# PEER experts of a two-layer decoder step: gathered rows, or both tables streamed through TensorE

## The reference

```python
q = (xt @ w_q).reshape(n, PEER_HEADS, 2, PEER_QDIM // 2)
s = jnp.einsum('nhcd,hckd->nhck', q, sub_keys).astype(jnp.float32)
s1, i1 = lax.top_k(s[:, :, 0], PEER_TOPK)
s2, i2 = lax.top_k(s[:, :, 1], PEER_TOPK)
...
top, sel = lax.top_k(cand, PEER_TOPK)
eidx = jnp.take_along_axis(cidx, sel, axis=-1)
gate = jax.nn.softmax(top, axis=-1)
...
a = jax.nn.gelu(jnp.einsum('nhkd,nd->nhk', u[ek], xk).astype(jnp.float32), approximate=False)
return jnp.einsum('nhk,nhkd->nd', (gk * a).astype(v.dtype), v[ek])
```

## Time and profile before

| | |
|---|---|
| median of 3 runs | 2763.49 us (2759.49 to 2781.48) |
| profiled execution, first to last instruction | 2750.8 us |
| PE busy | 2018.4 us (73%), 6651 matmuls |
| DVE busy | 1539.8 us (56%) |
| ACT busy | 415.0 us (15%) |
| POOL busy | 692.8 us (25%) |
| DMA | 759.36 MB, of which 608.21 MB by the gathers |
| mean granted TensorE clock | 0.828 |

### The profile page before, as it was taken

One profiled execution on the slowest core, in us unless ns is written; L12 is line 12 of the kernel. 1 busy time (PEld: TensorE's weight loads), 2 busy tenths in 40 slices (PEclk: granted clock), 3 DMA queues, 4 the chain that ended last, 5 costly groups with the idle time before them and its releaser, 6 DMA issues. The chain is left out here.

```text
span 2750.8 us, 21320 instructions
## 1 busy us (share of the span) xinstructions
PE 2018.4 (73%) x6651; PEld 989.5 (36%) x6651; DVE 1539.8 (56%) x3816; ACT 415.0 (15%) x1168; POOL 692.8 (25%) x612
## 2 busy tenths in 40 slices
PE   8956688895666867779786766776867767666766
PEld 3544446372122233334452332531223344222222
DVE  0063431377987453433559366488377647966665
ACT  0000231001111011111111122111123111111111
POOL 4000000002232222222232132233133424244542
PEclk9975565997888987778788988898988889888888
DMA  8201001437688897777887989997988999699997
GB/s 277 78 1 21 14 1 53 162 123 298 227 329 308 332 353 275 286 291 278 292 311 276 348 311 364 361 360 270 399 328 338 409 392 368 244 407 421 422 419 296
DMA packets 190137, 759.36 MB, mean 276 GB/s; under 512 B 22204, under 2 KB 79432, under 8 KB 116168
## 3 DMA queue, kind: packets, MB, share of 16 engines
q0 software_dynamic: 84480, 608.21, 56.5%
q1 hardware_dynamic: 105544, 149.80, 15.9%
HBM read 752.35 MB, written 5.60 MB: 276 GB/s over the span
## 5 line engine op out<-in xcount | busy, mean ns | idle before, releaser
L1750 PE MATMUL ps<-uv,diag 128*128 128x512 f32 (+1 forms) x1884 | 1059.4, 705 | 373.0 <-ACT diag L1726 339.7
L1638 POOL DMA_INDIRECT uv<-in_experts_dram,slots x576 | 662.2, 1150 | 1993.9 <-PE ps L1750 1332.6
L1658 DVE CUSTOM_DVE_ANT_0 uv<-uv,x 128x1024 f32<-128x1024 f32 x512 | 622.9, 1223 | 305.6 <-DMA uv<-in_experts_dram,slots 176.0
L1750 PEld LDWEIGHTS ps<-uv,diag 128*128 128x128 f32 (+1 forms) x1884 | 368.9, 210 | 940.3 <-ACT diag L1726 453.7
L1726 ACT ACTIVATE diag<-const,wgt 128x128 f32<-128x128 f32 (+1 forms) x471 | 164.2, 385 | 810.6 <-DVE wgt L1668 779.6
L1713 ACT ACTIVATE gelu<-dot 128x2 f32<-128x2 f32 x288 | 58.6, 203 | 673.7 <-DVE dot L1658 668.3
L1680 DVE SCALAR_TENSOR_TENSOR acc<-uv,wgt,acc 128x1024 f32<-128x1024 f32 x100 | 128.1, 1281 | 0.0
L421 PE MATMUL ps<-even_w,xT 128*128 128x512 f32 (+3 forms) x240 | 96.9, 559 | 0.9 <-DMA even_w<-in_even_w_in_dram 0.9
L1658 DVE CUSTOM_DVE_ANT_0 uv<-uv,xs 128x1024 f32<-128x1024 f32 x64 | 78.3, 1226 | 29.1 <-DMA ffn_gb<-in_ln_ffn_b_dram 14.0
L704 PE MATMUL ps<-sample_s_kTs,sample_s_q_b 64*32 64x256 f32 x256 | 62.2, 414 | 43.9 <-DVEq L1782 43.9
L421 PEld LDWEIGHTS ps<-even_w,xT 128*128 128x128 f32 (+1 forms) x240 | 37.5, 163 | 59.9 <-issue 56.1
(11 more groups left out here) (414 smaller groups left out, 2109.5 us busy)
## 6 DMA issues: line engine op xcount, KB each, us to landing
uv<-in_peer_w_q_dram SPq DMA_DIRECT2D x16, 1024.0 KB, 11.9
sample_cache<-in_cache_dil_kv_dram SPq DMA_DIRECT2D x64, 256.0 KB, 8.6
sample_cache<-in_odd_w_in_dram SPq DMA_DIRECT2D x12, 1024.0 KB, 8.5
first_w<-in_odd_w_in_dram SPq DMA_DIRECT2D x12, 1024.0 KB, 9.6
last_w<-in_odd_w_in_dram SPq DMA_DIRECT2D x12, 1024.0 KB, 13.0
uv<-in_experts_dram,slots POOLq DMA_INDIRECT x576, 8.9
even_w<-in_even_w_in_dram SPq DMA_DIRECT2D x8, 1024.0 KB, 8.6
sample_w<-in_peer_w_q_dram SPq DMA_DIRECT2D x8, 1024.0 KB, 13.9
```

Of the source, the lines that this page charges most:

```text
L1638: self.k.nc.gpsimd.indirect_dma_start(out=self.uv[:, s % RING, :], out_offset=None, in_=self.table, in_offset=bass.IndirectOffsetOnAxis(ap ...
L1658: ins = nc.vector.tensor_tensor_reduce(self.uv[:, s % RING, 0:D], self.uv[:, s % RING, 0:D], x, 1.0, 0.0, ALU.mult, ALU.add, self.dot[:, g ...
L1750: last = nc.tensor.matmul(k.bank(c)[0:m, :], self.diag[:, s % RING, 0:m], self.uv[:, s % RING, D + 512 * c:D + 512 * (c + 1)], start=(j == ...
```

## The change

Nothing is gathered any more and no work stands beside the experts. For each layer `experts_after` does the output projection with its norm, the transposition of x and the queries of all 288 tokens, each alone, and then `expert_layer` computes **all** 16384 experts for **all** 288 tokens, with the gates of the experts that a token did not choose at zero. `second_mixer` now runs alone between the two expert layers, with all tokens at once. The constants that only the mixers need are loaded again ahead of each of them (`mixer_constants`), because the SBUF is needed in between for the array `shares` (128 x 128 x 288 f32: for each second choice the partition, then first choice, then token).

`expert_layer` has three passes over PE:

1. For each of 128 blocks of 128 rows u (512 KB, one DMA from SP, ring of 4): eight transpositions into two banks, two copies of 128x512 by ACT, eight matmuls with 288 moving columns that give 128 experts x 288 tokens, and the gelu of them by ACT into `shares`. DVE does the routing of all three tiles meanwhile. PE turns block b before it multiplies block b-1.
2. For each token a matrix of 128 x 128 gates: POOL makes a one-hot of the token's first choices (128 slots x 128), DVE a one-hot of the second choices times the gates, PE multiplies the two. For four tokens at a time (a *quad*, 72 of them) DVE multiplies the four matrices into `shares`. Two quads of one-hots are buffered (`HOT`), four banks hold products (`M_BANKS`).
3. For each of 128 blocks of rows v (512 KB): eight matmuls with 288 moving columns, one for each 128 columns of v, added up over all blocks in the eight banks. Then the result is copied out, turned back, and normed.

```diff
-RING = 8
+RING = 4
+HOT = 2
+QUAD = 4
+QUADS = NTOK // QUAD
+M_BANKS = (4, 5, 6, 7)
...
+            def turn(b):
+                pe.wait_ge(landed[b % RING], 16 * (b // RING + 1))
+                for h in range(2):
+                    if b:
+                        pe.wait_ge(evicted, 2 * (b - 1) + h + 1)
+                    for c in range(4):
+                        last = nc.tensor.transpose(k.bank(h)[:, 128 * c:128 * (c + 1)],
+                                                   buf[:, b % RING, 128 * (4 * h + c):128 * (4 * h + c + 1)], ident)
+                    last.then_inc(turned, 1)
+
+            def dots(b):
+                pe.wait_ge(evicted, 2 * (b + 1))
+                if b >= 2:
+                    pe.wait_ge(gelued, b - 1)
+                for c in range(KC):
+                    last = nc.tensor.matmul(k.bank(2 + b % 2)[:, 0:NTOK], uT[:, b % 2, 128 * c:128 * (c + 1)], k.xT[:, c, :],
+                                            start=(c == 0), stop=(c == KC - 1))
+                last.then_inc(dotted, 1)
...
+            for q in range(QUADS):
+                pe.wait_ge(firsts, QUAD * (q + 1))
+                pe.wait_ge(seconds, QUAD * (q + 1))
...
+                for j in range(QUAD):
+                    last = nc.tensor.matmul(k.bank(M_BANKS[q % len(M_BANKS)])[:, 128 * j:128 * (j + 1)], hot[:, q % HOT, 1, j, :],
+                                            hot[:, q % HOT, 0, j, :], start=True, stop=True, skip_group_check=True)
+                last.then_inc(spread, 1)
+            pe.wait_ge(gelued, NK)
+            pe.wait_ge(shared, QUADS)
+            for b in range(NK):
+                pe.wait_ge(landed[(NK + b) % RING], 16 * ((NK + b) // RING + 1))
+                for c in range(KC):
+                    last = nc.tensor.matmul(k.bank(c)[:, 0:NTOK], buf[:, (NK + b) % RING, 128 * c:128 * (c + 1)], G[:, b, :],
+                                            start=(b == 0), stop=(b == NK - 1))
+                last.then_inc(used, 1)
...
+                    nc.gpsimd.tensor_scalar(hot[:, q % HOT, 0, j, :], iota, lists[:, 0, n:n + 1], None, ALU.is_equal).then_inc(firsts, 1)
...
+                        nc.vector.tensor_scalar(hot[:, q % HOT, 1, j, :], iota, lists[:, 1, n:n + 1], lists[:, 2, n:n + 1],
+                                                ALU.is_equal, ALU.mult).then_inc(seconds, 1)
...
+                    nc.vector.tensor_tensor(some, some, gates, ALU.mult).then_inc(shared, 1)
```

More of the change, by code:

```diff
@@ L59 @@
 SLOTS = PH * PK
-RING = 8
-GROUP = 2
-LAG = 3
 LEVELS = (1, 2, 4, 8, 16, 32, 64)
@@ L1555 @@
-ORDER = (2, 0, 1)
-VISITS = [(layer, t) for layer in range(DEPTH) for t in ORDER]
-STEPS = [SLOTS // 4 if t == 2 else SLOTS for _, t in VISITS]
-FIRST = [sum(STEPS[:i]) for i in range(len(STEPS) + 1)]
-WINDOWS = (
-    ("route 0 0", FIRST[0], ()),
-    ("route 0 1", FIRST[1], ()),
-    ("mixer 2", FIRST[1] + 30, (3,)),
-    ("route 1 2", FIRST[2] + 16, ()),
-    ("mixer 0", FIRST[2] + 46, (3,)),
-    ("route 1 0", FIRST[3] - 16, ()),
-    ("mixer 1", FIRST[3] + 16, (3,)),
-    ("route 1 1", FIRST[5] - 34, ()),
-    ("nothing", FIRST[5], (3,)),
-)
@@ L1777, in side_ticks @@
-def side_ticks(k, stages, name, eng, ended, base):
-    for n, stage in enumerate([Stage(k, 0)] + stages):
-        yield from stage.run(name, eng)
-        eng.drain().then_inc(ended, 1)
-        yield
-        eng.wait_ge(ended, 4 * (base + n + 1))
-        yield
-def experts_and_side_work(k, experts, windows):
-    ended = k.sem("side_stage_ended")
-    spans = []
-    for i in range(len(windows)):
-        spans.append((windows[i][0], windows[i + 1][0] if i + 1 < len(windows) else experts.ticks))
-    def both(name, eng):
-        main = {"tensor": experts.tensor, "vector": experts.vector, "scalar": experts.scalar}[name](eng)
-        base = 0
-        for (a, b), (_, stages) in zip(spans, windows):
-            side = side_ticks(k, stages, name, eng, ended, base) if stages else iter(())
-            weights = [0.5] * 2 + [w for st in stages for w in st.weights + [0.5] * 2] if stages else []
-            base += len(stages) + 1 if stages else 0
-            reached = np.cumsum(weights)
-            done = 0
-            for n in range(b - a):
-                next(main)
-                while done < len(weights) and (n == b - a - 1 or reached[done] * (b - a) <= reached[-1] * (n + 1)):
-                    next(side)
-                    done += 1
-            for _ in side:
-                raise AssertionError("side work left over")
-        for _ in main:
-            raise AssertionError("steps left over")
-    with k.nc.Block() as block:
@@ new lines, in expert_layer, with _ @@
+    out, back, normed, variance, rooted = [k.sem(name, n) for n in ("yT_out", "y_back", "normed", "variance", "rooted")]
+    z, stats = buf[:, 2, :], hot[:, 0, 0, 0, 0:16]
+    with nc.Block() as block:
+        @block.scalar
+        def _(act):
+            for c in range(KC):
+                nc.scalar.copy(k.xT[:, c, :], k.bank(c)[:, 0:NTOK]).then_inc(out, 1)
+            for n, r in enumerate(ROWS):
+                act.wait_ge(variance, n + 1)
+                nc.scalar.activation(stats[0:r, 15:16], stats[0:r, 14:15], ACT.Sqrt).then_inc(rooted, 1)
@@ L1849, in _ @@
-            experts.stores(sp)
-def dilated_tile(k, name, t, a, o, val, kT):
-    r, tiles = ROWS[t], (t,)
-    stages = [transpose_x(k, name + "_x", tiles, SIDE_BANKS)]
-    with ExitStack() as outer:
+            if store:
+                for t, r in enumerate(ROWS):
+                    sp.wait_ge(normed, t + 1)
+                    dst = store[0][0, 128 * t:128 * (t + 1), :] if t < 2 else store[1].rearrange("b t d -> (b t) d")
+                    k.store(sp, dst, k.x[0:r, t, :])
+                k.wait_for_stores(sp)
@@ new lines, in second_mixer, with _ @@
+            alone(k, values_load, attention(k, "dil_p", prompt_items(k, qT, kT, val, catT, 7), bufs, (0, 2), (4, 5)))
+        q_b = k.sbuf("dil_q_b", [128, HP, DEC_B, NS], ctx=ctx)
+        bufs = attention_buffers(k, "dil_s", PAST + NS, 128, ctx)
+        spread = Stage(k, 1)
+        @spread.on("vector")
+        def _(dve):
+            for c in range(HP):
+                last = k.nc.vector.tensor_tensor(q_b[:, c], bc(qT[:, c, SMP], 1, DEC_B), k.c("batch_cols"), ALU.mult)
+            k.dve_steps(last)
+            dve.wait_ge(v_in, 16 * DEC_B)
+            yield
@@ L1997, in build @@
-            with ExitStack() as second:
-                val = k.sbuf("dil_val", [128, TILES, D], ctx=second)
-                kT = k.sbuf("dil_kT", [128, HP, NTOK], ctx=second)
-                for t, name in zip(ORDER, ("sample", "first", "last")):
-                    work[f"mixer {t}"] = dilated_tile(k, name, t, a, o, val, kT)
-                    late, work[f"route 1 {t}"] = late_routing(k, name, t, a, r)
-                    work[f"mixer {t}"] += late
-            k.side = False
-            experts_and_side_work(k, experts, [(start, work[name]) for name, start, _ in WINDOWS])
+            mixer_constants(k, a["const"], ctx)
```

831 lines of the change are left out of this document (347 added, 484 removed).

## The result

The changed kernel takes 3812.3 us (median of 4 runs, 3805.99 to 3812.82); the kernel before, run beside it, 2766.8 us (4 runs). The ratio is 1.378, with a 95% interval of 1.374 to 1.383: 38% slower. The prediction was 2692 us, with a range of 2600 to 2840. The profiled execution of the changed kernel has a span of 3810.9 us, against a predicted span of 2679.

What follows compares the result with a forecast made beforehand. Bound before: a ring of eight 1 MB gathers together with side work on the same engines. New sum: 475 + 101 + 836 + 327 + 101 + 836 + 3 = 2679 us span, plus 12.7 to the median: 2692 us; range 2600 to 2840.

Steps and rivals of the forecast that it cites:

- the first price: Expert layer's f32 product with 288 moving columns on 128x128 weights: 0.243 us each, from 128 starts between 113.9 and 144.8 us.
- Pass 2: Gate spreading in the expert layer, 72 quads: 2.5 us a quad, 180 us a layer, with 149 and 245 us as ends.
- Second mixer: The mixer running alone between the expert layers: 327 us, including projection 62, prompt attention 57 and sample attention 125 plus 4.
- Transpositions: PE's 128x128 transpositions, eight a block in the expert layer's first pass: about 0.11 us each at clock 1.00.
- The page against this: Skill page says PE transpositions don't count as clock activity, endangering the first expert pass; the forecast said the trace disagrees.
- rival 2: Clock falls in the first expert pass: dense products take 18% more, 109 us a layer, 2910 us in all; chance 0.04.
- Hidden work of pass 1: ACT's copies and gelu (1.7 of 2.8 us a block), DVE's routing (190 us) and loads (186 GB/s) all hidden: cost 0.
- rival 3: Loads bound the third expert pass: landing 9.3 us, 2.8 us a block, 111 us more a layer, 2914 us; chance 0.05.
- lower bound: DVE's share of a quad in gate spreading: four one-hots at 0.345 us plus a 0.687 us multiplication, 2.07 us; 149 us.
- rival 1: POOL's one-hots bound gate spreading: gain gone from 0.75 us each; at 1.0 us each, 2908 us; chance 0.2.
- The range: 2600 to 2840 us for the whole kernel, said to hold the forecast, the lower-end case and most of the small-waits case.

## Why the prediction was wrong

**The step that failed** is the first price, as it went into the sum: "A product with 288 moving columns on 128x128 weights: 128 of them start between 113.9 and 144.8 us, so one each (144.8-113.9)/127 = 0.243 us". The division is right, and what it divides are 128 records of 64 products. So the bound engine's main term was taken at half its size: a product costs 0.486 us, as the run with half the products of pass 3 shows (507 us less, where 0.243 us would have given 249). The error went into every line that multiplied a number of products *from the program* by the price of a record: the queries, passes 1 and 3, "144 products of 512 columns, 62 us", and the "48 score products at 0.11 us". Terms that took their count *from a trace* (the sample attention's 256 and 512, the prompt attention, the first mixer) were not touched by it, nor were the transpositions, which are one record each. The half-size numbers looked sound because nothing checked the count of records against the program. That check was to be had. In the kernel before ACT writes one diagonal for each step of the two prompt tiles whose v PE adds, and PE makes two products with it:

```profile
L1726 ACT ACTIVATE diag<-const,wgt 128x128 f32<-128x128 f32 x411 | 148.0, 395 | 705.4 <-DVE wgt L1668 685.1 <-DVEq L1782 13.6 <-PE ps L1750 6.1
```

411 diagonals are 822 products, and the group row of L1750 has 1644 records: exactly two for a product.

The sum with the count put right, term by term (us):

| Term | predicted | measured | of it the count |
|---|---|---|---|
| First mixer and what precedes it | 475 | 480 | 0 |
| Output projection, norm, transpositions, twice | 134 | 132 | 0 |
| Queries, twice | 68 | 124 | +62 |
| First rows land, twice | 8 | 10 | 0 |
| Pass 1, twice | 734 | 1246 | +498 |
| Pass 2, twice | 360 | 335 | 0 |
| Pass 3, twice | 498 | 999 | +498 |
| End of a layer, twice | 72 | 65 | 0 |
| Second mixer | 327 | 420 | +62 |
| Last store | 3 | in the last end | 0 |
| Span | 2679 | 3811 | +1120 |

2679 + 1120 = 3799 of the measured 3811. (The measured terms are read from PE's starts in the timeline, the ends of layers are a little uncertain against what follows.) The 14 us that pass 1 still lacks are mostly the count again, in the score products of the routing: 48 a layer by the program, and 192 records in two layers, some 12 us a layer where 5.3 were priced:

```profile
L1493 PE MATMUL ps<-shares x192: 272/275/422, 614.4 to 2506.2; 128*128 128x128 f32 x128, 128*32 128x128 f32 x64
```

With 0.486 us for a product the same working would have given 2692 + 1120 = 3812 us. That this is the measured time to the microsecond is luck: beyond the count of the table the second mixer was priced 31 us too low and pass 1 14, pass 2 25 too high and the ends of the layers 7, and the 12.7 us that were added for the way from the span to the median are 1.4 here. With that price no change of this form could pay in f32: PE alone would need 2 x 128 x (16 x 0.486 + 8 x 0.11) = 2216 us for both layers' passes 1 and 3, more than the whole long block of before with its side work (2112).

What the other steps were worth:
- **Transpositions** 0.11 us: right (0.11). **The page against this**, rival 2: the granted clock is 1.00 over 617 us of pass 1, transpositions included, and the same without them. That alone settles little, since the products stand between, and what ran before the 3.4 us of transpositions at 1.00 could account for those. The second mixer of the changed kernel decides it: PE stands idle for 31 us and then does 176 transpositions and nothing else, from 2108.8 to 2130.1 us. In their first 3.2 us the clock is at the lower level, and it rises while PE does only transpositions:

```profile
2108.80:2112.00 3.20, 3.16 (x15) 3.19 (x16) 1.02 (x2) 0.58 (x1) 0.00 (x0) 0.50 0.00 0
2112.00:2116.00 4.00, 3.39 (x36) 3.14 (x34) 2.33 (x5) 2.29 (x5) 0.00 (x0) 0.94 0.00 0
2116.00:2130.10 14.10, 14.10 (x128) 13.91 (x128) 10.71 (x16) 8.79 (x15) 0.00 (x0) 1.00 0.01 2
```

The rule of the Trainium skill (TensorE: Matmul & The Clock Gate, Part 4: PE-mode transpose) that they don't count for the clock is not borne out here.
- **Hidden work of pass 1**: right. DVE is busy 173 us there (190 predicted) and then idle for 348 us until the lists are due, near 1139; ACT's copy 0.589 us as priced, its gelu 0.410 where I put an exponential's 0.535.
- **Loads**, rival 3: right that they are hidden, at 3.7 us a landing, even at twice the rate (half the products).
- **Pass 2**: 168 us for 180, by luck: two errors met. DVE's "lower bound" of 2.07 us was no bound (1.61). POOL's one-hot, taken as hidden or at most 0.85 us, is 0.58 us and sets the quad. That is the mechanism of rival 1, with the sign that was given for it (DVE waiting for PE, and PE for POOL), below the 0.75 us from which it would have eaten the gain.
- **Second mixer**: 420 us for 327, 62 us of it the count and the rest prices. The projection takes 129 us in place of 62; the sample attention, 2200 to 2354 us, 153 in place of 129; the prompt attention 66 in place of 57. Scores on 64 partitions are at the lower clock as forecast, and so are the value products, which I had priced from a stretch at a mixed clock: 44 us for 34. PE's timeline shows the projection, a burst of scores and one of values:

```profile
1948.68 129.09 PE L428 MATMUL ps<-odd_w,xT 128*128 128x512 f32 x288 [2.37 <-DMA odd_w<-in_odd_w_in_dram]
...
2286.06 7.04 PE L711 MATMUL ps<-dil_kTs,dil_q_b 64*32 64x256 f32 x18
...
2327.86 11.02 PE L736 MATMUL ps<-dil_s_probT,dil_raw 128*64 128x4 f32 x128
```

And the busy time of the first half of the sample attention shows the clock, 0.50, which is the lower level, with PE busy 99% of the time:

```profile
2200.00:2275.00 75.00, 74.47 (x227) 30.75 (x227) 4.78 (x14) 1.94 (x6) 0.00 (x0) 0.50 0.00 0
```

- **The range** left out the case that happened, since no rival put a price on a product: I gave bounds for the unknown instruction (POOL's one-hot, worth 65 us) and none for the instruction that made up 2000 us of PE's work.

## What to carry to other kernels

Before a price goes into a sum, divide the records of its row by the instructions that the program issues there: the price belongs to a record, the count of the sum to the program, and they must be of one kind. Give the term that is the largest part of the sum a second, independent reading, above all where the bound engine is the one that the change loads. And price a chain of short instructions by the distance of their starts, not by the length of their rows: rows of back-to-back work overlap, on PE and on DVE.
